# Gated merge kept in PSUM, one rounding of the down projection moved, and the second network's front reordered, in a two-network fp32 kernel

## The reference

```python
# first network, each layer (x: 256 latent tokens, xc: 256 context tokens; xc only in layer 0)
p = modulate(rmsnorm(x), sh1, sc1) @ w_in
y_conv = silu(layernorm(dwconv31(glu(p)))) @ w_conv_out
y_attn = neighbourhood_attention(q, k, v, k_ctx, v_ctx) @ w_na_out
x = x + g1 * ((sigmoid(pg1) * y_conv + sigmoid(pg2) * y_attn) @ w_out)      # the gated merge
u = dwconv3(modulate(rmsnorm(x), sh2, sc2) @ w_up)
x = x + g2 * ((silu(g) * a) @ w_down)                                       # (a, g) = halves of u
# second network, each layer (h: 16 meta tokens + 256)
proj = rmsnorm(h) @ w_in_2                     # qa ka va qi ki wi qb kb vb qc kc vc gc
score = sum_h wi * 8**-.5 * 64**-.5 * relu(qi_h . ki); idx = top_k(causal(score), 64)   # the indexer
a_out = attention on the chosen keys; b_out = difference attention; c_out = silu(gc) * rms(retention)
h = h + concat(a_out, b_out, c_out) @ w_out_2
h = h + relu(rmsnorm(h) @ w_ff1) ** 2 @ w_ff2
return rmsnorm(h)[:, 16:]
```

## Time and profile before

| | |
|---|---|
| median of 3 runs | 2050.26 us (2049.57 to 2053.6) |
| the profiled execution's own time | 2054.98 us |
| its span in the trace | 2053.2 us |
| granted clock of PE, mean | 0.984 of full speed |
| PE busy | 1962.6 us (96%) |
| PEld busy | 1672.8 us (81%) |
| POOL busy | 1189.3 us (58%) |
| DVE busy | 1064.7 us (52%) |
| ACT busy | 891.4 us (43%) |
| DMA | 306.57 MB, mean 149 GB/s |

### The profile page before, as it was taken

One profiled execution on the slowest core, in us unless ns is written; L12 is line 12 of the kernel. 1 busy time (PEld: TensorE's weight loads), 2 busy tenths in 40 slices (PEclk: granted clock), 3 DMA queues, 4 the chain that ended last, 5 costly groups with the idle time before them and its releaser, 6 DMA issues.

```text
span 2053.2 us, 34443 instructions
## 1 busy us (share of the span) xinstructions
PE 1962.6 (96%) x12628; PEld 1672.8 (81%) x12628; DVE 1064.7 (52%) x1962; ACT 891.4 (43%) x1515; POOL 1189.3 (58%) x904
## 2 busy tenths in 40 slices
PE   6999999999999999898989999899999999999997
PEld 3766676778888878787889999787799998779997
DVE  3169785736343322688666750785743028656402
ACT  3211444334333322434546653546555344565533
POOL 2333232433544455364577988464688876749895
PEclk8999999999999999999999999999999999999999
DMA  9799231244623232243444657343365554326553
GB/s 390 281 343 335 71 93 62 72 125 77 164 86 102 83 102 92 73 146 99 135 124 145 183 181 232 134 125 95 103 182 174 179 166 158 120 75 193 185 185 103
DMA packets 115687, 306.57 MB, mean 149 GB/s; under 512 B 29672, under 2 KB 44392, under 8 KB 115316
## 3 DMA queue, kind: packets, MB, share of 16 engines
q1 hardware_dynamic: 112664, 298.06, 45.5%
q10 hardware_dynamic: 2908, 6.90, 1.8%
HBM read 300.19 MB, written 8.06 MB: 150 GB/s over the span
## 4 chain that ended last, share of the span: by engine, by line
PE 42%; issue 30%; POOL 17%; DVE 8%; ACT 2%; DMA 0%; POOLq 0%; ACTq 0%; DVEq 0%; SPq 0%
POOL w_lo L652 17%; PE bank L1170 12%; PE bank L1172 12%; PE bank L1171 12%; DVE bank L1884 1%; PE bank L1634 1%; PE bank L1635 1%; PE bank L1636 1%; DVE nb L1876 1%; DVE bank L1876 1%; ACT w_hi L693 1%; DVE nb L1884 1%; DVE u_lo L1884 1%; PE bank L1810 0%; DVE rinv L1876 0%
## 5 line engine op out<-in xcount | busy, mean ns | idle before, releaser
L652 POOL TENSOR_TENSOR w_lo<-raw,w_hi 128x512 fp32r<-128x512 f32 x884 | 1171.3, 1352 | 842.6 <-ACT w_hi L693 842.0
L693 ACT ACTIVATE w_hi<-raw 128x1024 fp32r<-128x1024 f32 x442 | 466.4, 1056 | 292.0 <-PE bank L1172 236.0
L1170 PE MATMUL bank<-h_hi,w_hi 128*128 128x256 f32 (+1 forms) x1280 | 434.9, 340 | 6.3 <-ACT V L702 2.4
L1171 PE MATMUL bank<-h_lo,w_hi 128*128 128x256 f32 (+1 forms) x1280 | 426.9, 334 | 0.0
L1172 PE MATMUL bank<-h_hi,w_lo 128*128 128x256 f32 (+1 forms) x1280 | 426.9, 334 | 0.0
L1170 PEld LDWEIGHTS bank<-h_hi,w_hi 128*128 128x128 f32 x1280 | 242.5, 189 | 54.1 <-issue 21.2
L1172 PEld LDWEIGHTS bank<-h_hi,w_lo 128*128 128x128 f32 x1280 | 242.5, 189 | 26.4
L1171 PEld LDWEIGHTS bank<-h_lo,w_hi 128*128 128x128 f32 x1280 | 242.7, 190 | 25.5 <-issue 0.2
L1170 PE MATMUL bank<-u_hi,w_hi 128*128 128x272 f32 (+1 forms) x736 | 211.9, 288 | 3.2 <-DVE u_lo L1884 3.2
L1171 PE MATMUL bank<-u_lo,w_hi 128*128 128x272 f32 (+1 forms) x736 | 209.7, 285 | 0.0
L1172 PE MATMUL bank<-u_hi,w_lo 128*128 128x272 f32 (+1 forms) x736 | 209.5, 285 | 0.0
(11 more groups left out here) (338 smaller groups left out, 3718.3 us busy)
## 6 DMA issues: line engine op xcount, KB each, us to landing
raw<-in_wstream SPq DMA_DIRECT2D x442, 512.0 KB, 3.5
ada_raw<-in_wada SPq DMA_DIRECT2D x96, 512.0 KB, 6.5
biash<-rpb_by_offset SPq DMA_DIRECT2D x64, 64.0 KB, 3.0
rpb_by_offset<-in_rpb SPq DMA_DIRECT2D x16, 224.0 KB
bias_by_distance<-vec ACTq DMA_DIRECT2D x1, 3264.0 KB
bias<-bias_by_distance SPq DMA_DIRECT2D x2, 1632.0 KB, 8.6
X<-in_x_in ACTq DMA_DIRECT2D x1, 2048.0 KB, 11.8
bias<-bias_by_distance SPq DMA_DIRECT2D x2, 864.0 KB, 6.0
```

Source lines behind the costliest of these rows:

```text
L652: i = pool.tensor_tensor(w_lo[:, s, part], raw[:, s, part], w_hi[:, s, part].bitcast(F32), ALU.subtract)
L693: act.activation(w_hi[:, s, :], raw[:, s, :], ACT.Copy).then_inc(sem("w_hi_ready"), 1)
L1170: pe.matmul(o, hi, a_hi, start=start, stop=False)
L1171: pe.matmul(o, hi, a_lo, start=False, stop=False)
```

## The change

It has four places.

1. Gated merge: the second product and the sum are written in place in bank m % 4; `y_hi` and `y_lo` are made from that bank. Its reader for PE becomes `merge_lo` of chunk m.
2. Down projection, layer 0: `ahead` for slab 20 moves behind the copy of j = 21.
3. Second network's front, both layers: PE turns the unscaled `wi_t` and also one row of `rho` (four matmuls, bank 5) after slab `QCR + 1`; DVE scales the turned weights by the token's factor twice, after `("u", 0)`. ACT rounds slab s + 4 ahead of the copies of `KI`; the `sum` step of ACT comes one slab earlier; two `u` steps of ACT come later; in layer 1 `eager_chunks` ends bank by bank from k = 5 on. In layer 0 the 16 meta columns' square and rounding move from ACT to DVE and `meta_lo` behind the second chunk's output.
4. SP loads slabs front + 10 and front + 11 ahead of its wait for `fin1`.

```diff
-        L2_PLAN += [("sum", 0), ("slab", QI + 3), ("slab", QCR), ("wi", 0), ("slab", QCR + 1), ("index", 0), ("index", 1)]
+        L2_PLAN += [("sum", 0), ("slab", QI + 3), ("slab", QCR), ("slab", QCR + 1), ("wi", 0), ("index", 0), ("index", 1)]
...
         for st in L2_PLAN:
-            SCALAR_PLAN.append(st)
+            if st != ("sum", 0):
+                SCALAR_PLAN.append(st)
+            if st == ("slab", QI + 1):
+                SCALAR_PLAN.append(("sum", 0))
             if st == ("slab", QCR):
                 SCALAR_PLAN.append(("u", 0, 1))
             if st == ("index", 1):
-                SCALAR_PLAN += [("u", 0, 0), ("u", 1, 1)]
-            if st == ("slab", KCR):
-                SCALAR_PLAN.append(("u", 1, 0))
+                SCALAR_PLAN.append(("u", 1, 1))
+            if st in (("slab", KCR), ("slab", KCR + 1)):
+                SCALAR_PLAN.append(("u", st[1] - KCR, 0))
-        VECTOR_PLAN = [("rho", 0), ("wi", 0), ("stream", 0), ("u", 0), ("index", 0), ("index", 1), ("u", 1), ("index", 2), ("index", 3)]
+        VECTOR_PLAN = [("rho", 0), ("stream", 0), ("u", 0), ("wi", 0), ("index", 0), ("index", 1), ("u", 1), ("index", 2), ("index", 3)]
...
-            loads(front + 10)
+            loads(front + 12)
             sp.wait_ge(*after("fin1", DC - 1))
...
-                    copy(y_hi[:, m, 0:T], nr[:, m % 2, 0:T]).then_inc(*done("merge_hi", (layer, m)))
+                    copy(y_hi[:, m, 0:T], bank[m % 4][:, 0:T]).then_inc(*done("merge_hi", (layer, m)))
...
                         if j >= 2:
-                            ahead(s_down + min(j, FF_C - 2))
+                            ahead(s_down + j - (j >= FF_C - 2))
...
                 if layer == 0:
-                    act.wait_ge(*after("meta_x", 0))
-                    act.activation(meta_sq.rearrange("p (c t) -> p c t", c=DC), H[:, :, 0:META], ACT.Square).then_inc(*done("meta_sq", 0))
-                    copy(v_hi[:, :, 0:META], meta_x).then_inc(*done("meta_hi", 0))
+                    act.wait_ge(*after("fng", 0))
...
                         if c == KI:
+                            ahead(s + 1)
                             copy(wi_t[64:72, :], lin[l2_bank(step)][64:72, META:T2]).then_inc(*done("wi_out", layer))
...
-                for k in range(3, 6):
+                one = (6, 5)[layer]
+                for k in range(3, one):
                     for b in range(4):
                         piece(b, k)
                 for b in range(4):
-                    for k in (6, 7):
+                    for k in range(one, DC):
                         piece(b, k)
...
-                    readers[b] = readers[m % 4] = ("merged", (layer, m))
+                    readers[b] = ("merged", (layer, m))
+                    readers[m % 4] = ("merge_lo", (layer, m))
...
-                        pe.wait_ge(*after("wi_ready", layer))
-                        claim(6)
+                        pe.wait_ge(*after("wi_out", layer))
+                        pe.wait_ge(*after("rho", layer))
+                        claim(5)
                         for i in range(2):
-                            mm = pe.matmul(aux[2][:, 8 * i:8 * i + 8], wi_t[64:72, i * P:(i + 1) * P], ident[64:72, 64:72],
+                            mm = pe.matmul(aux[1][:, 8 * i:8 * i + 8], wi_t[64:72, i * P:(i + 1) * P], ident[64:72, 64:72],
+                                           start=True, stop=True)
+                            mm = pe.matmul(aux[1][:, 16 + i:17 + i], rho[64:65, META + i * P:META + (i + 1) * P], ident[64:65, 64:65],
                                            start=True, stop=True)
-                        readers[6] = ("wi_scaled", layer)
+                        readers[5] = ("wi_scaled", layer)
...
-                    tt(y_lo[:, m, 0:T], nr[:, m % 2, 0:T], y_hi[:, m, 0:T].bitcast(F32), ALU.subtract)\
+                    tt(y_lo[:, m, 0:T], bank[m % 4][:, 0:T], y_hi[:, m, 0:T].bitcast(F32), ALU.subtract)\
...
-                    stt(nt[:, 1, 0:T], gates[:, 2 * m + 1, 0:T], 1.0, bank[m % 4][:, 0:T], ALU.add, ALU.mult)\
+                    both = bank[m % 4][:, 0:T]
+                    stt(both, gates[:, 2 * m + 1, 0:T], 1.0, both, ALU.add, ALU.mult)\
...
-                    tt(nr[:, m % 2, 0:T], nt[:, 0, 0:T], nt[:, 1, 0:T], ALU.add).then_inc(*done("merged", (layer, m)))
+                    tt(both, both, nt[:, 0, 0:T], ALU.add).then_inc(*done("merged", (layer, m)))
...
+                    tt(meta_sq.rearrange("p (c t) -> p c t", c=DC), H[:, :, 0:META], H[:, :, 0:META], ALU.mult).then_inc(*done("meta_sq", 0))
...
+                    dve.tensor_copy(v_hi[:, :, 0:META], meta_x).then_inc(*done("meta_hi", 0))
                     dve.wait_ge(*after("meta_hi", 0))
-                    dve.wait_ge(sem("slab_used"), first["l2", 0] - 1)
-                    tt(v_lo[:, 0:6, 0:META], meta_x[:, 0:6, :], v_hi[:, 0:6, 0:META].bitcast(F32), ALU.subtract).then_inc(*done("meta_lo", 0))
...
+                    if eager and m == 1:
+                        dve.wait_ge(sem("slab_used"), first["l2", 0] - 1)
+                        tt(v_lo[:, 0:6, 0:META], meta_x[:, 0:6, :], v_hi[:, 0:6, 0:META].bitcast(F32), ALU.subtract).then_inc(*done("meta_lo", 0))
...
-                        dve.wait_ge(*after("wi_out", layer))
-                        tt(wi_t[64:72, :], wi_t[64:72, :], rho[64:72, META:T2], ALU.mult).then_inc(*done("wi_part", layer))
-                        dve.wait_ge(*after("wi_part", layer))
-                        tt(wi_t[64:72, :], wi_t[64:72, :], rho[64:72, META:T2], ALU.mult).then_inc(*done("wi_ready", layer))
...
-                        ts(wis, aux[2][:, 0:16], IDX_HEADS ** -0.5 * 64 ** -0.5, ALU.mult).then_inc(*done("wi_scaled", layer))
+                        ts(token_rho[:, 0:2], aux[1][:, 16:18], 1.0, ALU.mult).then_inc(*done("wi_part", (layer, 0)))
+                        ts(token_rho[:, 2:4], aux[1][:, 16:18], IDX_HEADS ** -0.5 * 64 ** -0.5, ALU.mult).then_inc(*done("wi_part", (layer, 1)))
+                        dve.wait_ge(*after("wi_part", (layer, 1)))
+                        for i in range(2):
+                            ts(wis[:, 8 * i:8 * i + 8], aux[1][:, 8 * i:8 * i + 8], token_rho[:, i:i + 1], ALU.mult,
+                               token_rho[:, 2 + i:3 + i], ALU.mult).then_inc(*(done("wi_scaled", layer) if i else done("wi_part", (layer, 2))))
```

More of the change, by code:

```diff
@@ L117, in build @@
     GROUP.update({n: "front_step" for n in ("fng", "meta_x", "meta_lo", "meta_sum", "rho_part", "rho_arg", "rho", "ki_scaled",
-                                            "wi_part", "wi_ready", "r1", "r2", "tabs")})
+                                            "meta_sq", "meta_hi", "wi_part", "r1", "r2", "tabs")})
     seen = {}
@@ L288, in build @@
         meta_x = nb[:, 3, 0:DC * META].rearrange("p (c t) -> p c t", c=DC)
+        token_rho = small[:, 124:128]
         meta_sq = nb[:, 2, 0:DC * META]
```

## The result

The changed kernel takes 2034.62 us (median of 6 runs, 2034.53 to 2037.66), the kernel before 2049.91 us in the same comparison (2047.57 to 2053.6). The ratio is 0.9928, with a 95% interval of 0.9917 to 0.9939: 15.3 us less. The forecast was 2034.0 us. The sum was right; of its four terms two were near and two were wrong in opposite directions, as the places show.

What follows compares the result with a forecast made beforehand. PE bounds the kernel, busy 96% of the span. 6.3 + 6.1 + 0.9 + 3.2 = 16.5 us off the profiled 2054.98 gives 2038.5; that execution lay 4.7 above the median, so 2033.8, say 2034, range 2030 to 2038.

Steps and rivals of the forecast that it cites:

- (a): Layer 0's down projection: PE's wait for `dn_end` and the slow clock behind it go, 6.3 us.
- (b): Layer 1's gated merge: with PSUM operands DVE no longer holds PE, and the slow stretch goes, 6.1 us.
- (c): Second network's front, layer 0: old waits go, a new one at bank 5 comes; 0.9 us, bounds -6 and 7.5.
- (d): Second network's front, layer 1: earlier fifth slab, no slow stretch or `wi_t` wait; 3.2 us, bounds 1 and 4.8.
- my upper bound: Down projection: 6.3 us, wait and slow clock both gone; the lower bound was 3.3, the clock falling anyway.
- the four chunks take 3.03 each: Layer 1's merge: four chunks from 1037.18 to 1049.32 take 3.03 us each, and would take PE's 2.85.
- The new wait: Front, layer 0: PE stands 4.2 us at bank 5 for `wi_scaled` before starting `index` 2.
- the stream: Front, layer 0: DVE's eight `stream` instructions, seven at 1.3 us beside POOL and one at 0.4, 1308.9 to 1318.4.
- Rival 1: Front, layer 0: DVE keeps up as the stream runs partly clear of POOL; 6.6 us more, 2027; chance 0.22.
- the move of the meta columns' work: Front, layer 0: square and rounding go from ACT to DVE; put at nothing, either way 0.5 us.
- rival 2: One term fails: in-place PSUM operations are dear, or the bank 5 wait grows by 5 us; 2040; chance 0.16.
- rival 4: Front, layer 0: the bank 5 wait makes the kernel slower, from 20 us more on (2055); chance 0.04.

Runs made afterwards that it cites:

- load_only: The kernel before, with only SP's loads of slabs front + 10 and front + 11 put ahead of its wait for `fin1`: 2047.95 us, ratio 0.9994.
- u_merge: The changed kernel with the gated merge in SBUF again: 2038.24 us, ratio 0.9934.
- x_both: The changed kernel with the stream's factor in PSUM bank 4 and DVE's scaling of the indexer's weights ahead of `u` 0: 2030.93 us, ratio 0.9908.
- u_load: The changed kernel with SP loading only up to slab front + 9 ahead of its wait for `fin1`: 2043.28 us, ratio 0.9954.
- x_wi: The changed kernel with DVE's scaling of the indexer's weights ahead of `u` 0 in both layers: 2035.52 us, ratio 0.9930.
- y_order: The changed kernel with the stream's factor in PSUM, layer 0's scaling ahead of `u` 0, tables and first rope ahead of `index` 2 and 3: 2028.94 us.

## Why the prediction was right, and where its terms were not

Us gained by the lead, in the two executions of the old code (the profile before, and `load_only`), and with the part undone:

| place | forecast | profile before | load_only | part undone |
|---|---|---|---|---|
| (a) down projection | 6.3 | 6.1 | 4.7 | 4.7 |
| (b) merge, layer 1 | 6.1 | 5.5 | 2.2 | 0.9 |
| (c) front, layer 0 | 0.9 | 3.6 | (early load in it) | 3.5 |
| (d) front, layer 1 | 3.2 | 3.5 | 3.6 | 5.1 |

The numbers of (b) are taken behind the next norm. The profile before holds 0.4 to 0.5 us for the slow stretch ahead of the merge; the two others do not have it.

(a) The mechanism was as forecast, the wait exact (3.19). The clock's part is 3.0 us in one execution and 1.5 in two others: my upper bound was the one case I had seen.

(b) This is the term that failed for an execution without the slow stretch. The step is "the four chunks take 3.03 each", taken with the wait of 3.56 us as what the SBUF merge costs. Every profile of it has `y_lo` at 1.37 us on average, yet the wait is 3.56 us in one and 1.28 in two, and in `load_only` the same four chunks take 2.89 each. What differs is a slow stretch of the clock ahead of the merge. With it, the sum meets POOL's pieces too (0.92 us on average, 0.60 in the others). With the whole merge in PSUM no wait follows, whether the slow stretch is there or not. So the edit was worth 0.9 and 2.2 us where the clock had not fallen there, and 5.5 where it had. Of the gross gain about 1.1 us is given back at the next norm, where two additions of `rinv` and `sq` meet a POOL piece and take 3.10 us; the kernel before and `u_merge` have 1.83. That is phase as well, and no price of PSUM: `load_only`, with the merge in SBUF, has 3.10 too. That the slow stretch is what sets the phase was seen in one execution against two, not forced by an experiment, and stays argued. The sentence of the Trainium skill on the fixed cycles of a PSUM read (VectorE: DVE Perf Modes, § The TRN2 errata) had no effect that can be seen: uncontended, `y_lo` for 512 columns takes 0.678 us from PSUM and 0.682 from SBUF, the sum 0.699 and 0.691, and over layer 0's merge the changed kernel and both executions of the old code agree within 0.1 us.

(c) The new wait was forecast at 4.2 and is 4.48, the stream at 1308.9 to 1318.4 plus waits and took 10.99 us; the second pair was to start 0.2 us earlier and started 1.25 earlier. Rival 1 is out. The mis-sized terms are two. The waits for `v_lo` in the eager slabs, 1.31 and 1.36 us before, are 0.2 and 0.55 after; I had put the move of the meta columns' work at nothing. All three profiles with that work unmoved have the long waits, and nine of the eleven with it moved the short ones; but `u_merge` and `x_both`, with it moved, waited 1.27 and 0.50, and 1.26 and 1.38. So the move mostly shortens them, and no experiment undoes it alone. And from the second pair to the slabs of values behind the waits, 2.3 us were gained where I had 0.7: the stand cost 1.7 us of clock where I had put 2.3, and the other 1.0 is not traced to a cause. The experiments add what the sum hid: in the new order the early load is worth 7.5 us, in the old one 3.4. Without it, in `u_load`, this place is thus 7.5 - 3.6 = 3.9 us slower than in the kernel before, by the lead of one profile each: part 3 is a loss in layer 0 until part 4 is there.

The rule of the Trainium skill on a DVE instruction with two SBUF inputs beside GpSimd (SBUF — State Buffer, § Who interferes with whom) carried the new wait in (c), and the runs agree with it: 1.508 us against 0.474 with one operand moved.

(d) As forecast: the wait for the fifth slab and that for `wi_t` are gone, 3.5 us against 3.2; with the part undone `wi_t` was waited for 2.2 us, not 0.63, hence 5.1.

**The sum** was right because errors cancelled, and that was luck. Against its own execution (2054.98 us) the forecast was 16.5 us, and the changed kernel's profiled one (2034.59) is 20.4 below: 18.7 of it at the four places, where (c) was 2.7 too small, and the rest in steps elsewhere. Against the median the gain is 15.3. I had taken the 4.7 us by which that execution lay above the median for something elsewhere. But `load_only` has 1.4 us less than it at (a) and 3.3 less at (b), 4.7 together of the 6.8 us by which the two executions differ beside the early load (10.2 by the lead at the end, less 3.4); and `load_only`'s own 2044.98 + 3.4 = 2048.4 lies near the median. The profiled execution was slow largely at the places that the change mends, and an execution like `load_only`'s had less to gain: 4.7 at (a), 2.2 at (b), 3.6 at (c) (its early load's 3.4 and 0.2) and 3.6 at (d), 14.1 us together, near the measured 15.3. So (a) and (b) were too large by 5.5 us for such an execution, (c) and (d) too small by 3.1, and what was left nearly met the median. Of rival 2, (b) did mostly fail on such an execution, though not by the price of PSUM; rival 4 did not come.

## What to carry to other kernels

Before costing a stall from one profile, ask what put the loop in that phase: here the same merge code waited 1.3 us in two executions and 3.6 in the one that had a slow clock just ahead of it. Where DVE is late beside a busy GpSimd, give each of its instructions one PSUM operand before reordering them; here one redirected reciprocal took 7.8 us off eight instructions, of which PE's wait got 2.7, as the next instructions met POOL in their place; reordering alone (`x_wi`) only moved the wait, and reordering on top of it (`y_order`) removed it. Before moving work in an engine's order, look for a load behind which it will now stand: the same order was a gain of 3.6 us with two slabs loaded early and a loss of 3.9 without.

## What the runs showed that I had not expected

A stand of PE does not always bring the clock down, nor always by as much. Behind the same stand of 3.19 us the clock over the next 6.3 us was 0.53 in one execution and 0.77 in two others. Behind the same stand for `V` near 932 us (2.4 us) the changed kernel kept 1.00 in one profile and fell to 0.85 over 7.5 us in another, both of identical code:

```profile
934.00:940.00 6.00, 5.29 (x32) 3.72 (x30) 5.18 (x12) 2.44 (x6) 2.13 (x2) 1.00 0.24 87
```
```profile
934.00:941.50 7.50, 6.87 (x36) 5.07 (x35) 5.17 (x12) 2.36 (x6) 2.19 (x2) 0.85 0.17 64
```

By the lead that is a step of 1.5 us. Two more, of 1.4 us each, stand near 1785 and 1840 us, the other way round: there the clock was 0.83 over 10 us in the first profile and 1.00 in the second. The six runs of this kernel lie within 3.1 us of each other, and within 6.3 us on a second chip; a few such places could make up much of that, which no run here tests.
